# A hybrid decoder layer on one core: projections from the unnormalized input, scaled afterwards, and another order in the compression stage

## What is computed

```python
def rms_norm(x, gain):
    xf = x * lax.rsqrt(jnp.mean(x * x, axis=-1, keepdims=True) + EPS)
    return xf * gain

h = rms_norm(x, norm_mix[l])
(hq, hf, hi, hg, nq, kc, vc, ksl, vsl, kwn, vwn, ngate, gate_a, gate_b) = jnp.split(h @ w_in[l], offsets, axis=-1)
y_a = hgrn2_mixer(hq, hf, hi, hg, lower_bounds[l], hg_out_gain[l]) @ w_branch_a[l]
y_b = nsa_mixer(nq, kc, vc, ksl, vsl, kwn, vwn, ngate, ...) @ w_branch_b[l]
mixed = jax.nn.sigmoid(gate_a) * y_a + jax.nn.sigmoid(gate_b) * y_b
x = x + mixed @ w_out[l]
h = rms_norm(x, norm_mlp[l])
x = x + jnp.square(jax.nn.relu(h @ w_up[l])) @ w_down[l]
```

## Time and profile before

| | us |
|---|---|
| median of 3 runs | 833.63 (832.14 to 833.74) |
| profiled execution | 835.81 |
| its span, first to last instruction | 834.0 |
| TensorE busy | 799.5 (96%) |
| VectorE busy | 377.9 (45%) |
| ScalarE busy | 196.8 (24%) |
| GpSimd busy | 499.5 (60%) |

### The profile page before, as it was taken

The page is one execution under the profiler, slowest core; times in us unless marked ns, Lnnn a source line. Parts: engine busy times, 40 slices in busy tenths (PEclk is TensorE's granted clock), DMA queues, the critical chain, the costliest instruction groups (busy, mean ns, idle before and its releaser), DMA issues.

```text
span 834.0 us, 12223 instructions
## 1 busy us (share of the span) xinstructions
PE 799.5 (96%) x4592; PEld 632.1 (76%) x4592; DVE 377.9 (45%) x532; ACT 196.8 (24%) x408; POOL 499.5 (60%) x326
## 2 busy tenths in 40 slices
PE   1899999998999999999999999999999999999998
PEld 0588876886878756666887888888888888888886
DVE  4853175651325344452787766664000276660000
ACT  3310233221431255564412222221000022220000
POOL 4566654376544555565665656676666677666663
PEclk9999999999999999999999999999999999999999
DMA  7134321123242210002432333223333222333320
GB/s 257 36 101 145 138 97 55 58 97 125 74 154 77 76 51 26 27 26 66 162 101 78 99 102 101 84 92 101 101 101 98 83 96 101 101 101 118 111 98 25
DMA packets 22972, 77.98 MB, mean 94 GB/s; under 512 B 2660, under 2 KB 2924, under 8 KB 22805
## 3 DMA queue, kind: packets, MB, share of 16 engines
q1 hardware_dynamic: 18864, 68.69, 24.9%
q10 hardware_dynamic: 4068, 8.75, 3.0%
HBM read 75.31 MB, written 4.21 MB: 95 GB/s over the span
## 4 chain that ended last, share of the span: by engine, by line
PE 92%; DVE 3%; POOL 1%; DMA 1%; ACT 1%; issue 1%; SPq 0%; DVEq 0%; POOLq 0%; ACTq 0%
PE bank L353 26%; PE bank L354 25%; PE bank L355 25%; PE bank L653 3%; PE bank L665 3%; PE bank L686 2%; PE bank L403 1%; PE bank L405 1%; PE bank L404 1%; PE bank L377 1%; PE bank L579 1%; DMA x<-in_xT 1%; DVE hf L1098 1%; POOL wsp L290 1%; PE bank L450 1%
## 5 line engine op out<-in xcount | busy, mean ns | idle before, releaser
L290 POOL TENSOR_TENSOR wsp<-wraw,wsp 128x1024 fp32r<-128x1024 f32 x127 | 313.6, 2469 | 10.6
L288 POOL TENSOR_SCALAR wsp<-wraw 128x1024 fp32r<-128x1024 f32 x127 | 141.4, 1114 | 262.5 <-PE bank L355 167.1
L353 PE MATMUL bank<-hhi,wsp 128*128 128x512 f32 x352 | 143.6, 408 | 9.6 <-POOL wsp L290 4.6
L354 PE MATMUL bank<-hlo,wsp 128*128 128x512 f32 x352 | 139.2, 395 | 0.0
L355 PE MATMUL bank<-hhi,wsp 128*128 128x512 f32 x352 | 139.2, 395 | 0.0
L353 PE MATMUL bank<-ghi,wsp 128*128 128x512 f32 x256 | 100.4, 392 | 0.0
L355 PE MATMUL bank<-ghi,wsp 128*128 128x512 f32 x256 | 99.8, 390 | 0.0
L353 PE MATMUL bank<-uhi,wsp 128*128 128x512 f32 x256 | 99.7, 389 | 0.0
L354 PE MATMUL bank<-glo,wsp 128*128 128x512 f32 x256 | 99.7, 389 | 0.0
L355 PE MATMUL bank<-uhi,wsp 128*128 128x512 f32 x256 | 99.6, 389 | 0.0
L354 PE MATMUL bank<-ulo,wsp 128*128 128x512 f32 x256 | 99.6, 389 | 0.0
(11 more groups left out here) (220 smaller groups left out, 978.9 us busy)
## 6 DMA issues: line engine op xcount, KB each, us to landing
wraw<-in_w SPq DMA_DIRECT2D x127, 512.0 KB, 3.3
x<-in_xT SPq DMA_DIRECT2D x4, 512.0 KB, 6.0
bias_skewed<-bias_lines ACTq DMA_DIRECT2D x1, 2048.0 KB
bias<-bias_skewed ACTq DMA_DIRECT2D x1, 2048.0 KB, 9.2
x<-in_xT ACTq DMA_DIRECT2D x1, 2048.0 KB, 9.6
out<-x ACTq DMA_DIRECT2D x8, 256.0 KB, 2.0
cst<-in_w ACTq DMA_DIRECT2D x1, 96.0 KB
ohs<-in_oh ACTq DMA_DIRECT2D x1, 82.5 KB
```

The lines of the kernel that those rows point to most:

```text
L288: pool.tensor_scalar(whi[:, two, :], wraw[:, raw, :], 1.0, 0.0, ALU.mult, ALU.add).then_inc(w_hi, 1)
L290: pool.tensor_tensor(wlo[:, two, :], wraw[:, raw, :], whi[:, two, :].bitcast(F32), ALU.subtract).then_inc(w_split, 1)
L353: pe.matmul(out_, wh, mh, start=first, stop=False)
L354: pe.matmul(out_, wh, ml, start=False, stop=False)
```

## The change

- x times the norm's gain is split instead of h. ScalarE writes hhi with the gain as its scale, VectorE writes hlo = x * gain - hhi in one operation per tile. The tile hf is gone, and GpSimd's share of hlo too.
- The reciprocal root (rx, and r_tok, one value per token on the partitions) multiplies the results. Channel-major results are multiplied on VectorE when they are read from the bank (`first_output`, `scaled`); i and m results get r_tok as the scale of ScalarE's reading. kc and vc go to SBUF first, and ScalarE places blocks from there.
- The statistics of x move on TensorE into the third projection (f1), with four narrow matmuls for r_tok. f0, q0, f1 and q1 use banks 0 to 3. Sixteen matmuls on ones (`WARM`) stand first.
- The first weight chunk is loaded before x; GpSimd splits the second in two halves.
- In the compression stage `level_256` for all heads follows hidden(0,0), and mixed_values(0) and (1) stand behind hidden(0,1) and hidden(1,0).
- gb6 stands behind step 30 instead of 25.

```diff
-GB_AFTER = {1: "gb2", 7: "gb3", 13: "gb4", 19: "gb5", 25: "gb6", 33: "gb7"}
+GB_AFTER = {1: "gb2", 7: "gb3", 13: "gb4", 19: "gb5", 30: "gb6", 33: "gb7"}
...
-        users = ["stat_x"] + users + ["kc", "vc", "ks", "kw", "st_ks", "nq0", "st_kw", "nq1", "st_q0", "nq2", "st_q1",
+        users = ["f2", "q2", "f3", "q3"]
+        users = users + ["kc", "vc", "ks", "kw", "st_ks", "nq0", "st_kw", "nq1", "st_q0", "nq2", "st_q1",
...
+            load(0, 0)
             for n in range(4):
                 sp.dma_start(x0[:, 2 * n:2 * n + 2, :], xT[:, 2 * n:2 * n + 2, :]).then_inc(x_in[n], 16)
-                if n >= 2:
-                    load(n - 2, n - 2)
-            for c in range(2, FIRST):
+            for c in range(1, FIRST):
...
-                    for k in range(1, KT, 2):
-                        pool.wait_ge(h_hi, k + 1)
-                        pool.tensor_tensor(hlo[:, k, :], hf[:, k % 4, :], hhi[:, k, :].bitcast(F32),
-                                           ALU.subtract).then_inc(lo_ready[1], 1)
...
+            def x_stat(k):
+                if k != 2:
+                    return
+                stat("stat_x", ones[:], xsq[:, 0, :], to=bank[5])
+                for t in range(ST):
+                    last = pe.matmul(bank[4][:, 2 * t:2 * t + 2], xsq[:, 0, t * P:t * P + P], ones[:, 0:2],
+                                     start=True, stop=True)
+                last.then_inc(tok_stat, 1)
...
             pe.wait_ge(set_up, 3)
-            stat("stat_x", ones[:], xsq[:, 0, :])
+            for n in range(WARM):
+                pe.matmul(bank[7][:, 0:P], ones[:], ones[:], start=True, stop=True)
+            first_projection(0, x_split)
+            first_projection(1, w_half)
             pe.wait_ge(consts_in, 16 * N_CONSTS)
...
+            first_projection(2, x_stat)
+            first_projection(3, lambda k: None)
...
+                for k in (2 * n, 2 * n + 1):
+                    act.activation(hhi[:, k, :], x0[:, k, :], ACT.Copy, scale=g_mix[:, k:k + 1]).then_inc(x_hi, 1)
+            for n in range(4):
                 act.activation(xsq[:, 2 * n:2 * n + 2, :], x0[:, 2 * n:2 * n + 2, :], ACT.Square).then_inc(x2_sq, 1)
...
+            for k in range(KT):
+                dve.wait_ge(x_hi, k + 1)
+                dve.scalar_tensor_tensor(hlo[:, k, :], x0[:, k, :], g_mix[:, k:k + 1], hhi[:, k, :].bitcast(F32),
+                                         ALU.mult, ALU.subtract).then_inc(x_lo, 1)
...
+            def scaled(name, to):
+                dve.wait_ge(w_used, AT[name] + 1)
+                link(dve.tensor_tensor(to, bank_of(name)[:], rx[:], ALU.mult))
+                dve.sem_inc(free[USE[name] % 2], 1)
...
+            raw("kc", kc_raw[:], blocks_in)
             keep_own(0)
             positions(0)
+            raw("vc", vc_raw[:], blocks_in)
             keep_own(1)
             positions(1)
             blocks_low(0)
             blocks_low(1)
+            raw("ks", ksn[:], raw_copied)
...
+                if n < 5:
+                    raw(("kw", "nq0", "nq1", "nq2", "nq3")[n], (kwn[:], *(qn[:, i, :] for i in range(4)))[n], raw_copied)
...
-            project("g0")
-            pe.wait_ge(tok_copied, 8)
-            hidden(0, 0)
-            level_256((0, 1))
-            project("g1")
-            level_256((2, 3))
-            hidden(0, 1)
-            project("g2", each_k=lambda k: fold_hidden(0) if k == 2 else None)
-            hidden(1, 0)
...
+            project("g0")
+            pe.wait_ge(tok_copied, 8)
+            hidden(0, 0)
+            level_256()
+            project("g1")
+            hidden(0, 1)
...
             mixed_values(0)
+            fold_hidden(0)
+            project("g2")
+            hidden(1, 0)
             mixed_values(1)
+            pe.wait_ge(gel_ready, 1)
+            to = claim("cmp_k")
+            pe.matmul(to[:, 0:64], w2_k, gel[0], start=True, stop=True).then_inc(cmp_out, 1)
+            project("g3")
+            hidden(1, 1)
+            stat("st_kc", pair_ones[:], hid[:, 7, :], 64)
             fold_hidden(1)
             project("ga0")
...
+                if t in GB_AFTER:
+                    gate(GB_AFTER[t])
```

More of the change, by code:

```diff
@@ L370, in _, with stat, first_projection @@
             stats = [0]
-            def stat(name, matrix, squares, n=S):
+            def stat(name, matrix, squares, n=S, to=None):
                 stats[0] += 1
                 pe.wait_ge(stat_in, stats[0])
-                to = claim(name)
+                to = claim(name) if to is None else to
                 pe.matmul(to[:, 0:n], matrix, squares, start=True, stop=True).then_inc(stat_out, 1)
+            def first_projection(n, each_k):
+                if n == 1:
+                    wh, wl = whi[:, 1, :], wlo[:, 1, :]
+                else:
+                    wh, wl = take(CHUNKS[n])
+                for k in range(KT):
+                    each_k(k)
+                    c = slice(k * P, k * P + P)
+                    last = three(bank[n][:], wh[:, c], wl[:, c], hhi[:, k, :], hlo[:, k, :], k == 0, k == KT - 1)
+                last.then_inc(w_used, 1)
@@ L386, in h_split @@
-            def h_split(k):
-                pe.wait_ge(lo_ready[k % 2], k // 2 + 1)
-            for h in range(HG):
-                project(f"f{h}", each_k=h_split if h == 0 else None)
-                project(f"q{h}")
+            pe.matmul(bank[6][0:NH, 0:512], relx[:], ohs[:, 0:512], start=True, stop=True).then_inc(bias_line, 1)
+            pe.matmul(bank[7][0:NH, 0:P], relx[:], ohs[:, 512:TW], start=True, stop=True).then_inc(bias_line, 1)
+            first_projection(2, x_stat)
+            first_projection(3, lambda k: None)
@@ L393, in token_major @@
+            for h in range(2, HG):
+                for n, name in enumerate((f"f{h}", f"q{h}")):
+                    if h == 2:
+                        pe.wait_ge(first_out, n + 1)
+                    project(name)
             def token_major(names, tiles, cols):
@@ L489, in level_128, with level_256 @@
                     last.then_inc(sc_done, 1)
-            def level_256(hs):
+            def level_256():
                 pe.wait_ge(decayed, 9)
-                for h in hs:
-                    to = sc_bank()
+                for h in range(HG):
+                    to = sc_bank() if h < 2 else bank[h]
                     for j in range(2):
@@ L551, in fold_hidden @@
                 last.then_inc(folded, 1)
-            project("g0")
-            pe.wait_ge(tok_copied, 8)
-            hidden(0, 0)
-            level_256((0, 1))
-            project("g1")
-            level_256((2, 3))
-            hidden(0, 1)
-            project("g2", each_k=lambda k: fold_hidden(0) if k == 2 else None)
-            hidden(1, 0)
-            pe.wait_ge(gel_ready, 1)
-            to = claim("cmp_k")
-            pe.matmul(to[:, 0:64], w2_k, gel[0], start=True, stop=True).then_inc(cmp_out, 1)
-            project("g3")
-            hidden(1, 1)
-            stat("st_kc", pair_ones[:], hid[:, 7, :], 64)
-            for n in range(2):
-                pe.wait_ge(sc_kept[n], 8)
-            pe.wait_ge(near_placed, 1)
             def mixed_values(h):
@@ L1238, in _, with gate_g, gelu @@
             link(dve.reciprocal(gate3, gate3))
-            for j in range(2):
+            def gate_g(h):
+                scaled(f"g{h}", gs[:, h, :])
+                dve.sem_inc(gs_out, 1)
+            def gelu(j):
                 u_, t_, e_ = (hid[:, 3 * j + n, :] for n in range(3))
@@ L1263, in _, with gate @@
             dve.sem_inc(kcn_ready, 1)
+            gelu(1)
+            def gate(name):
+                scaled(name, gates[:, "ab".index(name[1]), int(name[2]), :])
+            gate("ga0")
             dve.wait_ge(g_sig, 1)
@@ L1334, in _ @@
                 c_weight(qb)
+                gate(("ga5", "ga6", "ga7", "gb0")[qb])
+            gate("gb1")
             def shift(t, g):
```

228 lines of the change are left out of this document (120 added, 108 removed).

## The result

The changed kernel takes 826.17 us (median of 4 runs, 826.07 to 826.28), the kernel before 833.68 beside it (832.14 to 833.77): a ratio of 0.9916, 95% interval 0.9905 to 0.9928. It is faster, by 7.5 us where 14.3 were forecast, and 1.7 above the upper end of the range.

What follows compares the result with a forecast made beforehand. TensorE, busy 799.5 of 834.0 us, was taken as the bound, with only its idle and half-rate time to gain. -12.9 + 1.2 - 2.8 + 0.2 = -14.3 us gave 819.3 us as median, range 813.5 to 824.5.

Steps and rivals of the forecast that it cites:

- Term 1: Start, up to q1's end: the earlier start gives -12.9 us, with bounds of -15.5 and -10.
- Rival (a): VectorE's and GpSimd's turns fall well and ga0 starts at the high clock: -18.3, 815.3 us; chance 0.20.
- Term 2: From kc to nq1: VectorE, emptying banks in order, delays the decay step: +1.2 us, from 0 to +2.5.
- Term 3: Compression stage: the new order removes TensorE waits for GpSimd's split: -2.8 us, from -1.8 to -4.2.
- Term 4: Gates and attention: small waits for VectorE's products, one bank claim no longer waiting: +0.2 us, from -0.7 to +2.5.
- rival (b): TensorE's unexplained 1.8 us wait among 128 tiny matmuls goes, with the slow stretch behind it: 816.0 us; chance 0.11.
- Rival (c): VectorE's order costs more than seen, each bound at its worse end: -6.8, 826.8 us; chance 0.12.
- (d): f2 and all after wait for the root mean square and VectorE's heads, early start lost: 833.6 us; chance 0.03.
- (e): All 36 banks come free late because VectorE is busy; at 0.6 us each 840.9 us; chance 0.04.
- The conversion to the median: Whole kernel: the profiled execution lay 2.2 us above its median, so 819.3 us was forecast instead of 821.5.

Runs made afterwards that it cites:

- the two experiments: The changed kernel with the old order of the compression stage, 829.08 us; the kernel before with only the new order, 831.55 us.
- the unit stride: The changed kernel, but VectorE writes kc and vc to SBUF turned, so that ScalarE's block copies read consecutive floats: 818.76 us.
- the decay step first: The changed kernel, but VectorE makes ks's product and the first decay step ahead of positions(1) and both blocks_low: 821.51 us.

## Why the prediction was wrong, point by point

**Term 1, the start: right.** -12.9 forecast, -12.9 in the trace (q1 read at 37.26). The worked chain held to within a microsecond, with some luck in the last step: chunk 2 came 0.9 earlier than forecast, and f1 and q1 then took 13.0 us (24.27 to 37.26) where 12.4 were worked out. f0's first matmul came at 9.12 (9.35 forecast), the hlo chain from 8.22 with 0.7 a step, chunk 1's second half was ready at 19.5 (20.0), chunk 2 at 24.2 (25.1). VectorE and GpSimd do take turns; the last experiment of the start shows it with the additions moved away, and that whatever is gained at one chunk is lost at the next. Rival (a)'s luck did not come. What I credited to the warm-up matmuls' high clock is nothing: without them q1 comes 0.1 later.

**Term 2, VectorE's order: wrong, and this is the step that failed.** It said +1.2, at most +2.5. Measured from q1 to the statistic of kw: +8.0, of which 1.8 on the way to the statistic of ks and 6.2 behind it. The place was as written, near_level(1) waiting for VectorE; nq0, which was to wait as well, did not. The error is in "ScalarE's block copies start 1.0 us later": the copies' start was counted (vc's come 1.3 later), and their length was taken over from the kernel before. But the change had moved their source from a bank to SBUF, which makes them 0.63 instead of 0.37 each, 2.1 us for the eight of vc and as much for those of kc. That was an operation with a new operand, and the prediction's own rule, a price from the nearest row, was not applied to it. The delay then did two more things for which the bound had no room. It put three operations of VectorE beside GpSimd's split (3.7 us more than in the run with fast copies, 2.9 more than in the kernel before), and it made the wait one behind which the clock fell, worth about 2; the mean clock was 0.994 to 0.996 in all four runs. With the copies made fast, TensorE loses 0.8 us from q1 to the statistic of kw (37.07 and 114.72), where the term said 1.2: 0.33 of it is the wait ahead of f3 for a bank that VectorE now reads. So the slow copies are what the term lacked, and nothing else of its size. Two groups of copies, each 2.1 us longer, cost 8.5 in all, 0.9 of it through a wait that no run explains. With them made fast the kernel is at 817.7, 1.6 below the forecast of 819.3, and within its range.

**Term 3, the compression stage: the mechanism right, the size a little off.** -2.8 forecast (its own pieces, -4.1 and +1.4, make -2.7), -3.6 in the traces, -2.9 and -2.1 by the two experiments. The waits came as worked out: none ahead of g1 and g2, 0.37 ahead of g3 (0.25 forecast), 0.40 at the fold (0.5), 1.54 ahead of ga0 (1.65). The low clock that was to come behind ga0 did not come in the four runs of the kernel after. Behind the same wait in other kernels it did come: in the profiled runs of the unit stride and of the bank given back by ScalarE, where two of the four times are 1.65 longer. A forecast should have said "sometimes 1.6". The 3.6 of the traces contain such a stretch in the profiled execution of before.

**Term 4, gates and attention: right.** +0.2 forecast, +0.3 in the traces from ga0 to the end. The products take 0.68 to 0.72 each, as priced. That ScalarE loses 22 us was too much: its busy time fell by 11. The slow copies gave 4.2 back, and the four exponentials of f stayed with it.

**The unexplained wait** of rival (b) stayed, at 1.6 instead of 1.8, but without the slow stretch behind it; from the statistic of kw to that of nq3 the kernel after gains 1.6. Those 1.6 stand in no term of the forecast. With the fast copies the wait is 0.7 to 0.8, and 0.2 with the decay step first. What it is stays open.

**Rival (c)** is what happened: 826.8 worked out, 826.17 measured. It had the right place, but its number came from all four terms at their worse ends, while in fact one term lay far beyond its own bound. It had a chance of 0.12. (d) and (e) did not come: nowhere else do the 36 banks come back late enough to matter.

**The conversion to the median** was off as well. I took 2.2 off, the distance of one execution from its median. The profiled run of before had two low stretches, at 146 to 152 (clock 0.88, 0.50, 0.77) and at 202 to 206, and its median run one by the mean clock. How many the new kernel has is a question of its own waits, not of the old ones.

**The miss, added up.** The forecast of the span was 819.7, measured were 824.2: 4.5 more. Term 2 gives +6.8, the stretch from the statistic of kw to that of nq3 -1.6, term 3 -0.8 and term 4 +0.1. The other 2.4 between 819.3 and 826.17 are the 2.2 that were taken off, for the new median lies 0.1 from its profiled execution, and 0.2 of time outside the span. Without the 2.2 the range would have ended at 826.7, just beyond the measured time, and term 2 would have been as wrong as it is.

## What to carry to other kernels

When a change gives an operation another source or target, price that operation anew, even if its line of code reads the same: here a copy with a strided read took 0.37 us from PSUM and 0.63, 1.7 times as much, from SBUF. Where engines hand work over with no slack, a delay is not paid once: it shifts what follows beside another engine's traffic and can drop the matrix engine's clock, so that twice 2.1 us became 8.5. And a wait of 1.5 us on TensorE is worth more than its length: filling it with useful matmuls that must run anyway also removed a stretch at half rate that came in some executions only.

## What the runs showed of the hardware

- ScalarE, a copy of 64x248 floats: 0.37 us from PSUM at a stride of 64 bytes, 0.63 from SBUF at that stride, 0.40 from SBUF at unit stride. VectorE writing 128x512 to SBUF with consecutive results 128 bytes apart: 1.12 instead of 0.68.
- TensorE's low clock behind a wait is not decided by the wait's length alone. Behind the same 1.54 us it came in the profiled run of one kernel and not of another, and the runs of that one kernel fall into pairs 1.65 apart. It came behind waits of 1.54, 1.55, 1.64, 1.81, 2.57 and 4.75, and did not come in other profiled runs behind 1.54, 1.60 and 2.40. Behind the waits of 0.9 to 1.1 of the profiled runs it was not seen. What else decides it is not shown.
- A VectorE operation of 1.2 us with two inputs in SBUF took 2.0 to 3.4 where GpSimd's split was under way, and 1.2 where it fell between two splits. A shift of 2 to 3 us of the same instructions decided it.
- Within a run of 128 tiny matmuls TensorE stood still for 0.2 to 1.8 us with nothing recorded that it waited for. The length differs between kernels. Among the changed ones it was 1.2 to 1.6 where near_level(1) had come late and 0.2 to 0.8 where it had not; in the two with ScalarE reading the banks, where it had not either, it was 1.8 and 1.3. No run here explains it.
